# One decoder layer on one core: where the 32 experts' weights, rows and outputs are placed and how they are moved

## The reference

```
h = rms_norm(x, norm2_w)
group = argmax(h @ w_group_router + b);  e1, e2 = the two best of the 8 experts of that group
w1, w2 = p(group) * softmax weights of e1, e2, divided by their sum
y = x + sum over the two of  w * (silu(h @ w_gate[e]) * (h @ w_up[e])) @ w_down[e]
```

## Time and profile before

| | |
|---|---|
| time, median of 3 runs | 1667.83 us (1662.85 to 1673.54) |
| time of the profiled execution | 1676.96 us |
| its span, first to last instruction | 1674.8 us |
| PE busy | 1388.8 us, 83% of the span |
| DVE, ACT, POOL busy | 394.4, 347.4, 59.9 us |
| read from and written to HBM | 386.58 MB, 35.78 MB |
| expert loop, first gate product to last down product | 1079.3 to 1641.0 us |

### The profile page before, as it was taken

How to read it: one execution, slowest core, us unless ns; L and a number is a source line. 1 busy time by engine, 2 the same in 40 slices (tenths; PEclk the granted TensorE clock), 3 DMA queues, 4 the chain that set the end, 5 groups by cost and what they waited for, 6 DMA issues and landing times.

```text
span 1674.8 us, 22415 instructions
## 1 busy us (share of the span) xinstructions
PE 1388.8 (83%) x8868; PEld 817.7 (49%) x8868; DVE 394.4 (24%) x693; ACT 347.4 (21%) x561; POOL 59.9 (4%) x116
## 2 busy tenths in 40 slices
PE   7999889869999998866999997298878877777781
PEld 5847444646667675545888754033333322333230
DVE  2012343333344344420111134010100110001003
ACT  2122323225454445640000011000000000000000
POOL 3000000020000002000000000100000000000002
PEclk9999999989999989997999998598898888888886
DMA  5129500027999989996610004699999999999985
GB/s 204 65 73 406 163 0 0 0 81 277 352 336 350 357 317 386 385 378 215 224 50 1 13 5 167 260 380 398 388 392 388 393 375 369 371 375 365 369 319 174
DMA packets 127495, 423.82 MB, mean 253 GB/s; under 512 B 16097, under 2 KB 24290, under 8 KB 115106
## 3 DMA queue, kind: packets, MB, share of 16 engines
q1 hardware_dynamic: 110850, 384.35, 62.0%
q0 software_dynamic: 7856, 28.45, 4.9%
q10 hardware_dynamic: 8688, 9.62, 1.8%
HBM read 386.58 MB, written 35.78 MB: 252 GB/s over the span
## 4 chain that ended last, share of the span: by engine, by line
PE 67%; issue 9%; DMA 8%; SPq 6%; DVE 6%; ACT 3%; POOL 1%; ACTq 0%; POOLq 0%; DVEq 0%
PE ps L1035 16%; PE ps L885 7%; PE ps L1056 6%; PE ps L582 6%; PE ps L708 4%; PE ps L585 4%; PE ps L888 4%; PE ps L943 3%; SPq L344 3%; DMA arena<-in_cache_k 3%; PE ps L719 2%; SPq L336 2%; PE ps L1022 2%; PE ps L741 2%; DMA arena<-in_w_gate_exp 1%
## 5 line engine op out<-in xcount | busy, mean ns | idle before, releaser
L1035 PE MATMUL ps<-arena 128*64 128x512 f32 x512 | 283.3, 717 | 110.4 <-issue 109.5
L1036 PE MATMUL ps<-arena 128*64 128x512 f32 x512 | 283.8, 718 | 0.0
L1035 PEld LDWEIGHTS ps<-arena 128*64 128x64 f32 x512 | 80.7, 164 | 275.9 <-issue 274.6
L708 PE MATMUL ps<-ident,arena 128*128 128x128 f32 x1024 | 148.8, 291 | 28.8 <-DMA arena<-in_cache_k 23.8
L708 PEld LDWEIGHTS ps<-ident,arena 128*128 128x128 f32 x1024 | 117.3, 147 | 99.1 <-issue 65.7
L1250 ACT ACTIVATE arena<-ps 128x512 f32<-128x512 f32 x192 | 108.4, 595 | 173.7 <-PE ps L708 173.7
L1851 DVE COPY arena<-ps 128x512 f32<-128x512 f32 x32 | 22.1, 692 | 437.3 <-PE ps L1022 437.3
L582 PE MATMUL ps<-mixers,arena 128*128 128x272 f32 x512 | 120.6, 397 | 0.5 <-DVE mixers L1399 0.5
L885 PE MATMUL ps<-mixers,arena 128*128 128x272 f32 x512 | 120.7, 397 | 0.0
L1056 PE MATMUL ps<-arena 128*64 128x512 f32 x256 | 116.7, 598 | 0.5 <-DVE arena L1866 0.5
L1057 PE MATMUL ps<-arena 128*64 128x512 f32 x256 | 116.7, 598 | 0.0
(11 more groups left out here) (299 smaller groups left out, 1315.9 us busy)
## 6 DMA issues: line engine op xcount, KB each, us to landing
arena<-in_cache_k SPq DMA_DIRECT2D x256, 256.0 KB, 5.1
arena<-in_cache_v SPq DMA_DIRECT2D x256, 256.0 KB, 5.2
arena<-in_w_gate_exp SPq DMA_DIRECT2D x32, 2048.0 KB, 21.4
arena<-in_w_up_exp SPq DMA_DIRECT2D x32, 2048.0 KB, 26.9
arena<-in_w_down_exp SPq DMA_DIRECT2D x32, 2048.0 KB, 28.6
arena<-in_w_in SPq DMA_DIRECT2D x7, 2048.0 KB, 13.2
expert_rows<-mixers POOLq DMA_DIRECT2D x1, 12288.0 KB, 46.8
arena<-in_w_in SPq DMA_DIRECT2D x8, 1024.0 KB, 8.6
```

Source lines behind the costliest of these rows:

```text
L708: last = turn(ps[:, TURN + j % 2, P * c:P * c + P], kring[n % 3][:, j, P * c:P * c + P], ident[:, :])
L1035: mm(ps[0:BLK, 1 + u, :], xgT[:, u, k, :], wgv[u][:, k, :], start=k == 0, stop=k == KD - 1)
L1036: last = mm(ps[BLK:P, 1 + u, :], xgT[:, u, k, :], wuv[u][:, k, :], start=k == 0, stop=k == KD - 1)
```

## The change

The tables of rows in HBM are made differently, and buffers are placed anew. In detail:

- There are three sets of weight buffers. Set 0 is loaded during the gates, set 1 when the last branch product is done, and of set 2 gate and up when the mixing is done and down when the lists are. From n = 3 on, gate and up of n wait for `gate_up(n - 3)`, and down of n for `down(n - 3)`. The second copy of x comes into the place of the normalised input, after the last gate product that reads that.
- ACT scales the rows by their root and stores them by token (`expert_rows` is now 544 rows). `norm2_w` is multiplied in after the rows of two experts are turned (`cols_out(j)`). The load of `norm2_w` to all partitions is gone.
- Lists by place are made with products of two one-hot matrices: `in_pos` (the place within the expert) and `codes` (expert, times token number). This gives each place of each expert its token, or a number beyond the bounds.
- POOL gathers the rows of two experts with one indirect transfer (`rows_in`), and places each expert's outputs, half rows of 512, by token with another (`rows_out`). Places without a token have a number out of bounds and are skipped. The zeroing is gone.
- At the end SP loads the outputs by token with plain transfers, after its loop over the extra blocks. POOL has such a loop too.

```diff
+            def gate_up_weights(n):
+                w = n % 3
+                if n >= 3:
+                    sp.wait_ge(S("gate_up"), n - 2)
+                sp.dma_start(wgv[w], a["w_gate_exp"][0, n].rearrange("(p k) f -> p k f", k=KD)
+                             ).then_inc(S(f"w_gate_exp_{w}"), 16)
+                if n == 2:
+                    sp.wait_ge(S("mixed"), 2 * NT)
+                sp.dma_start(wuv[w], a["w_up_exp"][0, n].rearrange("(p k) f -> p k f", k=KD)
+                             ).then_inc(S(f"w_up_exp_{w}"), 16)
...
+            def down_weights(n):
+                w = n % 3
+                if n >= 3:
+                    sp.wait_ge(S("down"), n - 2)
+                sp.dma_start(wdv[w], a["w_down_exp"][0, n].rearrange("(p j) d -> p j d", j=FJ)
+                             ).then_inc(S(f"w_down_exp_{w}"), 16)
...
+            for k in range(4):
+                sp.dma_start(wo[k], w_out[:, k, :]).then_inc(S("w_out"), 16)
+            sp.dma_start(x2[4][0:TS, :], x_tok[4]).then_inc(S("x_loaded_4"), 16)
+            gate_up_weights(0)
+            down_weights(0)
             for q in range(2, KD // 2):
                 sp.wait_ge(S("branch_products"), 8 * (q - 1))
                 gate_loads(q)
...
+            sp.wait_ge(S("branch_products"), 4 * 6)
+            sp.dma_start(carve(19200, 4, D), w_out[:, 4:KD, :]).then_inc(S("w_out"), 16)
+            sp.wait_ge(S("branch_products"), 4 * 7 + 2)
+            for i in range(4):
+                sp.dma_start(x2[i], x_tok[i]).then_inc(S(f"x_loaded_{i}"), 16)
+            sp.wait_ge(S("branch_products"), 4 * KD)
+            gate_up_weights(1)
+            down_weights(1)
             sp.wait_ge(S("mixed"), 2 * NT)
-            for n in range(2):
+            gate_up_weights(2)
+            sp.wait_ge(S("h2_stored_0"), 48)
+            sp.wait_ge(S("h2_stored_1"), 32)
+            sp.wait_ge(S("list_sums"), 4)
+            down_weights(2)
+            for n in range(3, NE):
                 gate_up_weights(n)
                 down_weights(n)
...
+            sp.wait_ge(S("extra_table"), 1)
             sp.wait_ge(S("down"), NE)
             novf = sp.value_load(tab[0:1, NOVF:NOVF + 1], min_val=0, max_val=NOVF)
             with sp.Fori(0, NOVF) as i:
                 e = sp.value_load(tab[0:1, bass.ds(i, 1)], min_val=0, max_val=NE - 1)
                 with sp.If(i < novf):
                     sp.wait_ge(S("extra_products"), extra_stage(i, 0))
+                    sp.wait_ge(S("extra_stored"), i * 16 + 16)
+                    sp.dma_start(extra_i[:, :], extra_dram[:, bass.ds(i * 2, 2)]).then_inc(S("extra_loaded"), 16)
...
+            sp.wait_ge(S("out_stored_0"), 16 * NE // 2)
+            sp.wait_ge(S("out_stored_1"), 16 * NE // 2)
+            sp.wait_ge(S("extra_stored"), novf * 16 + 16)
+            outs = yg_dram.rearrange("(c h) d -> c (h d)", h=2).rearrange("(k t) d -> t k d", k=2)
+            for i, r in enumerate(ROWS):
+                sp.dma_start(yg[i][0:r], outs[P * i:P * i + r]).then_inc(S(f"y_loaded_{i}"), 16)
...
-            pool.wait_ge(S("projected"), QKV)
-            full = NBLK * BLK // P
-            pool.dma_start(xg_dram[0:full * P, :].rearrange("(n p) d -> p n d", p=P),
-                           flat(ybT)[:, 0:D].unsqueeze(1).to_broadcast([P, full, D])).then_inc(S("rows_zeroed"), 16)
-            pool.dma_start(xg_dram[full * P:NBLK * BLK, :], flat(ybT)[0:NBLK * BLK - full * P, 0:D]
-                           ).then_inc(S("rows_zeroed"), 16)
...
+            pool.wait_ge(S("mixed"), 2 * NT)
+            chain(nc.gpsimd.memset(flat(xg), 0.0))
+            chain.wait()
...
+            def rows_in(j):
+
+                if j >= 2:
+                    pool.wait_ge(S("rows_turned"), j - 1)
+                pool.indirect_dma_start(
+                    out=xg[:, j % 2, :], out_offset=None, in_=h2_dram,
+                    in_offset=bass.IndirectOffsetOnAxis(ap=load_i[:, j:j + 1].bitcast(U32), axis=0),
+                    bounds_check=T - 1, oob_is_err=False).then_inc(S(f"rows_{j % 2}"), 16)
+
+            def rows_out(n):
+
+                pool.wait_ge(S("y_act"), n + 1)
+                pool.indirect_dma_start(
+                    out=yg_dram, out_offset=bass.IndirectOffsetOnAxis(ap=store_i[:, n:n + 1].bitcast(U32), axis=0),
+                    in_=m_y[n % 2], in_offset=None, bounds_check=4 * T - 1, oob_is_err=False
+                ).then_inc(S(f"out_stored_{n % 2}"), 16)
+
+            pool.wait_ge(S("h2_stored_0"), 48)
+            pool.wait_ge(S("h2_stored_1"), 32)
+            pool.wait_ge(S("lists"), 1)
+            for j in range(3):
+                rows_in(j)
+            pool.wait_ge(S("lists"), 2)
+            for n in range(NE):
+                rows_out(n)
+                if n == 5:
+                    pool.wait_ge(S("extra_table"), 1)
+                    pool.dma_start(extra_dram, extra_lists[:, :]).then_inc(S("extra_stored"), 16)
+                if n % 2 == 0 and n // 2 + 3 < NPAIR:
+                    rows_in(n // 2 + 3)
...
-            pool.sem_inc(S("pool_passed"), 1)
-            for i in range(NT):
-                for k in range(2):
+                        out=xg[0:BLK, 0, :], out_offset=None, in_=h2_dram,
+                        in_offset=bass.IndirectOffsetOnAxis(ap=extra_i[0:BLK, 0:1].bitcast(U32), axis=0),
...
+            def listed_codes(out, codes):
+
+                for c in range(2 * NT):
+                    r = ROWS[c // 2]
+                    last = mm(out, in_pos[0:r, c, :], codes[0:r, c, :], start=c == 0, stop=c == 2 * NT - 1)
+                last.then_inc(S("list_sums"), 1)
+
+            pe.wait_ge(S("codes"), 1)
+            listed_codes(ps[:, 0, 0:NE], codes)
...
-            act.wait_ge(S("branch_products"), 4 * KD)
-            load(w2r[:, :], a["norm2_w"].to_broadcast([P, D]), "router_inputs")
             act.wait_ge(S("merged"), KD)
             act.wait_ge(S("route_zero"), 1)
...
+                act.wait_ge(S("row_scales"), p + 1)
+                fn(own, x2[i][0:r, :], ACT.Copy, scale=rstd2[0:r, i:i + 1]).then_inc(S("h2"), 1)
+                act.wait_ge(S("h2"), p + 1)
+                act.dma_start(h2_dram[P * i:P * i + r, :], own).then_inc(S(f"h2_stored_{p % 2}"), 16)
...
-            dve.wait_ge(S("router_inputs"), 96)
+            dve.wait_ge(S("router_inputs"), 80)
...
+            pairs = r_Ok.rearrange("p (a b) n -> p a b n", b=2)
+            sums = r_j.rearrange("p (a b) n -> p a b n", b=2)
+            chain(v.tensor_tensor(sums[:, 0:4], pairs[:, 0:4], each(ps[:, 7, 0:NE * 4], 4).unsqueeze(2).to_broadcast([P, 4, 2, NE]),
+                                  ALU.mult))
+            step(v.tensor_tensor(sums[0:TS, 4], pairs[0:TS, 4], ps[0:TS, 7, NE * 4:NE * 5].unsqueeze(1).to_broadcast([TS, 2, NE]),
+                                 ALU.mult))
+            step(v.tensor_reduce(r_RK, r_j, mybir.AxisListType.X, ALU.add))
+            step(v.tensor_tensor(r_over, r_tops.unsqueeze(1).to_broadcast([P, 2 * NT, KMAX]),
+                                 r_RK.unsqueeze(2).to_broadcast([P, 2 * NT, KMAX]), ALU.is_le))
+            step(v.tensor_reduce(r_m, r_over, mybir.AxisListType.X, ALU.add))
+            chain(stt(out=r_main, in0=r_m, scalar=0.5, in1=tcode, op0=ALU.is_lt, op1=ALU.mult))
+            step(stt(out=r_pos, in0=r_m, scalar=-float(BLK), in1=r_RK, op0=ALU.mult, op1=ALU.add))
+            chain(v.tensor_tensor(in_pos, qcol.unsqueeze(1).to_broadcast([P, 2 * NT, P]),
+                                  r_pos.unsqueeze(2).to_broadcast([P, 2 * NT, P]), ALU.is_equal))
+            chain(v.tensor_tensor(codes, r_Ok, r_main.unsqueeze(2).to_broadcast([P, 2 * NT, NE]), ALU.mult))
+            chain.wait()
+            dve.sem_inc(S("codes"), 1)
...
+            def indices(src, n, at):
+
+                t, c, u = l_t[:, 0:n], l_c[:, 0:n], l_u[:, 0:n]
+                step(v.tensor_scalar(t, src, 0.5, EMPTY, ALU.is_lt, ALU.mult))
+                step(v.tensor_tensor(c, t, src, ALU.add))
+                step(v.tensor_scalar(t, c, T + 0.5, -float(T), ALU.is_gt, ALU.mult))
+                step(stt(out=t, in0=t, scalar=-1.0, in1=c, op0=ALU.add, op1=ALU.add))
+                if at == 0:
+                    for e in range(2):
+                        hs = slice(BLK * e, BLK * e + BLK)
+                        last = v.tensor_copy(load_i[hs, 0:NPAIR], t[hs, e:NE:2])
+                        if e == 0:
+                            chain(last)
+                    last.then_inc(S("lists"), 1)
+                else:
+                    chain(v.tensor_copy(each(extra_lists[:, :], NOVF)[:, :, 0], t))
+                step(stt(out=u, in0=c, scalar=2.0, in1=upper.to_broadcast([P, n]), op0=ALU.mult, op1=ALU.add))
+                return v.tensor_copy(each(extra_lists[:, :], NOVF)[:, :, 1] if at else store_i[:, :], u)
+
             dve.wait_ge(S("list_sums"), 2)
-            step(v.tensor_copy(r_base[:, :], ps[:, 5, 0:NE]))
```

(39 more changed lines are left out.)

343 lines of the change are left out of this document (140 added, 203 removed).

## The result

The changed kernel takes 1598.01 us (median, 1595.86 to 1599.12), the kernel before, timed beside it, 1670.68 (1662.85 to 1680.79). The ratio is 0.9561 [0.9513, 0.9608]: 4.4% faster, where 1632 was forecast with a range of 1608 to 1660. The direction was right and the size wrong: the time lies outside the range.

What follows compares the result with a forecast made beforehand. The experts were taken to be bound by bytes. First product -16, set less and shorter periods about -28, end +8 made -36 us, off the median of 1667.8: 1632 us, range 1608 to 1660 (8 in 10).

Steps and rivals of the forecast that it cites:

- Step 5: Experts' stream: fewer row bytes shorten the period per expert from 18.3 to 17.5 us, bounds 18.3 and 17.2.
- Step 4: Experts' stream: with a third buffer set, one set less is streamed after `gate_up(0)`, a gain of 17 to 18 us.
- Step 2: Before the experts: sets 0 and 1 load early, hidden, but set 1 delays the router's small loads, +5 us, bounds 0 and 9.
- Step 3: Lists and rows between mixing and experts: first gate product at 1063 instead of 1079.3, bounds 1056 and 1070.
- Step 7: End: output loads stand behind SP's loop of empty turns, 20 to 21 us; +8 us, bounds +6 and +14.
- Steps 1 and 6: Zeroing gone at 120 to 160: 0 to 1.5 us, taken as 0. POOL's expert transfers, 0.96 us each of 17.5: covered.
- A: More is gained: router inputs in time, loop at its quick pace, period 17.2 us; 1617 us, chance 0.18.
- B: Experts and end: bytes saved don't show, period stays 18.3 us, loop takes 26; 1659 us, chance 0.16.
- C: Experts: POOL's placements and gathers delay the weights; over 1% slower from a 19.4 us period, 1716 at 20.5; chance 0.08.
- D: Gates: early loads aren't early, SP stands at a full queue, gates stretch by up to 16 us; 1648 us, chance 0.05.

Runs made afterwards that it cites:

- experiment 11: Experiment 9's kernel, but expert 12 alone loads 64 rows into 64 partitions as before; 1633.54 us, ratio 0.9734.
- experiment 6: Kernel before, with the rows of experts 3 to 31 loaded into the same 64 partitions from ACT's queue instead of SP's; 1651.8 us, ratio 0.9874.
- experiment 2: Kernel before, with rows loaded for the first two experts only, all others working on these; 1596.64 us, ratio 0.949.
- experiment 9: Kernel before, with 128 rows loaded per expert into all 128 partitions instead of 64 into 64; 1630.08 us against 1680.38, ratio 0.9719.
- experiment 5: Kernel before, with the same row bytes on the same queue loaded into 128 partitions of 2 KB; 1616.36 us against 1672.66, ratio 0.9649.
- experiment 10: Changed kernel with two sets of weight buffers and gate and up of n issued ahead of down of n - 1; 1599.12 us, ratio 0.9551.
- experiment 12: Experiment 8 (three sets) with down of n - 1 issued behind gate and up of n, from n = 4; 1561.75 us, ratio 0.9316.
- Experiment 4: Changed kernel, with SP waiting until the router's inputs have landed before issuing expert 1's weights; 1588.87 us, ratio 0.9441.
- Experiment 8: Experiment 4 with SP's loop of 17 turns skipped when there are no extra blocks; 1569.22 us, ratio 0.9379.
- experiments 1: Kernel before, without the stores of the experts' outputs and the waits for them; 1670.13 us against 1677.86, ratio 0.9952.

## Why the prediction was wrong

**Step 5 failed, the period.** It said: "I take 17.5 us. Bounds: 18.3 [...] and 17.2". 15.4 was measured. The term took the rate of before as given and let only the bytes change. 6.57 MB an expert at 426 GB/s are 15.4 us; the 6.82 of before would be 16.0. So bytes gave 0.6, as forecast, and 2.3 of the old 18.3 were no bytes at all: they are what a row load into 64 partitions cost beyond its own, 2.4 in experiment 11. That the two agree so well is partly luck, as the price was lower early in the stage before and higher late (experiment 6). Over some 29 loads, 2.3 makes 66 us. The experiments agree with that sum: experiment 2 should give 66 and 18 of bytes, 84 (81 by the medians, 79 in the stretch), experiment 9 should give 66 less 20 of added bytes, 46 (50 and 42), and experiment 5 the 66 (56 and 61). What the loads did was to slow other packets, so their own bytes and landing did not show it. I had noted 415 GB/s beside POOL's transfers, and used it only to argue that POOL does no harm, not to ask why the stage itself had 371.

**Step 4 was sized wrong too**, the third set: 17 to 18 us forecast, 7 by experiment 10. Its timing was right (`down(0)` 15.2 us after `gate_up(0)`, 15 forecast). By experiment 12 a third set is worth 13, not a whole period, and the changed order takes 8 of that back: the share is 0.66 from 1080 to 1100. Without this error the miss would have been larger.

**Step 2, the router**: +5 forecast, bound 9. Experiment 4 gives back 9 in the medians and 12 in the trace, so the trace is past the bound. I priced the landing of small loads in a full stream; the price was on ACT, whose own issues stood 4.2 and 8.4 us. The rule of the Trainium skill, page "DMA: Bandwidth & Descriptors", section "SWDGE vs HWDGE vs iDMA", had put the term near its upper bound, which is the better side; the turns it tells of are in no row here.

**Step 3 was right**: 30.1 us from the end of mixing to the first gate product, 29 forecast. The product came at 1072.8, not 1063: 8.8 of the 9.8 between them are the mixing's end, 13.8 late instead of 5, of which 1.8 lie ahead of the router, and 1.1 are this step's.

**Step 7 was right**: the end grew by 6, forecast 8; SP's loop took 19.2, forecast 20. Experiment 8 shows that 15 of them were on the path; the last placement would have held the end for the other 4.

**Steps 1 and 6** hold as far as seen, though no experiment was made on them. From 120 to 160 PE is busy 38.5 of 40 us with the zeroing and without, while the DMA share falls from 1.02 to 0.35. POOL's instructions for an expert take 0.97 to 1.19 us each, and it waits for ACT, not the reverse.

**The sum again.** The forecast was -16 at the start, -28 in the experts, +8 at the end. The start came 10 later than that (step 2, the end of mixing), the end 2 earlier, and the experts gave 49 more: 28 periods of 15.4 instead of 17.5 are 59, less 10 for the third set. That makes -77; the spans differ by 78.

**The rivals.** A had the sign and missed the mechanism (quicker loop, router in time). B, that the period stays at 18.3, is refuted: 15.4 us is what 6.57 MB take at 426 GB/s. C, that POOL's indirect transfers delay the weights, is refuted by the rate: 426 with them. By the Trainium skill's best guess, page "DMA: Bandwidth & Descriptors", section "Latency and other measured facts", on the DMA engines that share ports with GpSimd's rings, they would have been costly here; the rate of 426, next to experiment 2's 427 without them, shows no such cost in this stream. D did not occur: from 740 to 960 the waits in front of PE's gate products are 0.2 us in all, against 0.4 before.

**What stays open.** That the load into half the partitions slows the weights' packets is shown; why it does is not. It is not the source, nor the lower half's addresses, nor packets of 4 KB: experiment 9 keeps all three and adds the upper half. No run loads 64 rows into the upper half alone, or into every other partition. The output stores do not do it, by experiments 1 and 2, but they go in pairs, one out of each half. Nor do I know what spreads the packets of a row load along the stage before.

## What to carry to other kernels

A DMA share of 1.0 need not be a full rate: divide GB/s by the best window of the same trace, and if a stage stays below it, find the transfer behind which the rate drops before pricing anything by bytes. Where a small load must stand in a stream of large ones, try it into all 128 partitions, even if that means loading more: here twice the bytes cost 42 to 50 us less. And let small loads that something waits for be issued before a stream starts, as their engine can stand at the issue.

## What the runs showed of the hardware

- A load of 0.26 MB from HBM into 64 of 128 partitions, in a stream of 2 MB weight loads, cost 2.4 us beyond its bytes (426 GB/s to 306 and 339 for 10 us). The same bytes into 128 partitions, and twice the bytes, left 425 to 426. While that load's packets ran, the weights' 16 KB packets took 1.1 us on average instead of 0.62.
- One core's queues held 425 to 427 GB/s for 400 us (1100 to 1500 in the changed kernel), reads of 2 MB tensors with gathers and placements beside them; the weights' 16 KB packets took 616 ns then.
- ACT stood 4.2 and 8.4 us at the issue of small loads while 6.3 MB went through SP's queue; with the stream held back, the same two took 0.69 and 0.67.
- 17 empty turns of a loop with a register load on SP took 19.2 us with the register load ahead of them, 1.1 each, and leaving them out gave 15 back.
